# Second mixer: the softmax weights are scaled inside the turn, by a diagonal of reciprocal sums

## What is computed

```python
q = rmsnorm(q.reshape(B, S, N_HEADS, HEAD_DIM), q_gain)
k = rmsnorm(k.reshape(B, S, N_HEADS, HEAD_DIM), k_gain)
...
s = jnp.einsum('bqhd,bkhd->bhqk', qb, kb).astype(jnp.float32) * scale + bias
valid = (c * CHUNK + kpos - pad) >= 0
s = jnp.where(valid[None, None], s, NEG_INF)
p = jax.nn.softmax(s, axis=-1)
return jnp.einsum('bhqk,bkhd->bqhd', p.astype(vb.dtype), vb)
```

## Time and profile before

| what | value |
|---|---|
| median of 3 runs | 1830.04 us (1828.27 to 1830.62) |
| the profiled execution, its own time | 1829.55 us |
| its span | 1827.7 us |
| busy share: TensorE, weight load, VectorE, ScalarE | 96%, 70%, 50%, 33% |
| mean granted TensorE clock | 0.987 of full speed |
| second mixer's attention (from the first scores to the last values) | about 1342 to 1441 us |

### The profile page before, as it was taken

The page is one execution under the profiler, slowest core; times in us unless marked ns, Lnnn a source line. Parts: engine busy times, 40 slices in busy tenths (PEclk is TensorE's granted clock), DMA queues, the critical chain, the costliest instruction groups (busy, mean ns, idle before and its releaser), DMA issues.

```text
span 1827.7 us, 19981 instructions
## 1 busy us (share of the span) xinstructions
PE 1755.2 (96%) x8340; PEld 1274.3 (70%) x8340; DVE 920.1 (50%) x1311; ACT 599.1 (33%) x900; POOL 12.5 (1%) x22
## 2 busy tenths in 40 slices
PE   7999999998999999999989999999999999999998
PEld 6777887785454445343478888887877778888886
DVE  4667864634232323232444845734577444745634
ACT  4456434442111111110143323323355333323322
POOL 0000000000000000000000000000000000000000
PEclk9999999998999999999999999999999999999999
DMA  5222225525899999999932141242310142242331
GB/s 197 93 70 70 93 75 177 190 106 217 361 422 422 421 421 421 422 420 420 398 110 93 65 143 69 65 142 93 115 70 36 57 134 87 69 138 69 101 107 58
DMA packets 93167, 330.59 MB, mean 181 GB/s; under 512 B 6176, under 2 KB 15536, under 8 KB 68368
## 3 DMA queue, kind: packets, MB, share of 16 engines
q1 hardware_dynamic: 88784, 317.81, 45.6%
q0 software_dynamic: 1984, 7.25, 1.1%
q10 hardware_dynamic: 2304, 4.20, 0.6%
HBM read 322.94 MB, written 6.29 MB: 180 GB/s over the span
## 4 chain that ended last, share of the span: by engine, by line
PE 86%; DMA 5%; DVE 4%; ACT 4%; issue 1%; SPq 0%; DVEq 0%; ACTq 0%
PE PS L1503 11%; PE PS L1504 10%; PE PS L1505 10%; PE PS L1383 10%; PE PS L1499 5%; PE PS L1500 5%; PE PS L1501 5%; PE PS L1406 5%; PE PS L1478 3%; PE PS L1479 3%; PE PS L1477 3%; PE PS L1354 2%; DMA rawz<-in_w_up_experts 2%; PE PS L1355 2%; PE PS L1416 2%; PE PS L1576 2%
## 5 line engine op out<-in xcount | busy, mean ns | idle before, releaser
L2198 DVE TENSOR_TENSOR lo<-raw,hi 128x2048 fp32r<-128x2048 f32 (+2 forms) x142 | 254.2, 1794 | 317.8 <-ACT hi L1798 317.4
L1798 ACT CAST hi<-raw 128x1024 fp32r<-128x1024 f32 (+2 forms) x144 | 216.9, 1513 | 297.5 <-PE PS L1505 112.3
L1503 PE MATMUL PS<-xh_ffn,hi 128*128 128x512 f32 x576 | 225.0, 391 | 0.9 <-DVE SG L2409 0.9
L1505 PE MATMUL PS<-xh_ffn,lo 128*128 128x512 f32 x576 | 224.2, 389 | 0.0
L1504 PE MATMUL PS<-xl_ffn,hi 128*128 128x512 f32 x576 | 224.1, 389 | 0.0
L1383 PE MATMUL PS<-raw,XG 128*64 128x512 f32 x416 | 140.2, 601 | 5.0 <-DVE YL L2175 2.8
L1503 PEld LDWEIGHTS PS<-xh_ffn,hi 128*128 128x128 f32 x576 | 108.1, 188 | 23.6 <-issue 1.3
L1505 PEld LDWEIGHTS PS<-xh_ffn,lo 128*128 128x128 f32 x576 | 108.1, 188 | 22.5
L1504 PEld LDWEIGHTS PS<-xl_ffn,hi 128*128 128x128 f32 x576 | 108.2, 188 | 22.1
L2168 DVE TENSOR_TENSOR HF<-SG,PS 128x512 f32<-128x512 f32 x16 | 17.3, 1078 | 183.5 <-PE PS L1383 183.5
L1383 PE MATMUL PS<-rawz,XG 128*64 128x512 f32 x400 | 88.9, 593 | 2.9 <-DMA rawz<-in_w_up_experts 2.9
(11 more groups left out here) (481 smaller groups left out, 3499.1 us busy)
## 6 DMA issues: line engine op xcount, KB each, us to landing
raw<-in_w_in SPq DMA_DIRECT2D x26, 1024.0 KB, 5.1
raw<-in_w_gate_experts SPq DMA_DIRECT2D x26, 1024.0 KB, 15.6
raw<-in_w_up_experts SPq DMA_DIRECT2D x26, 1024.0 KB, 14.4
rawz<-in_w_up_experts SPq DMA_DIRECT2D x26, 1024.0 KB, 12.9
rawz<-in_w_down_experts SPq DMA_DIRECT2D x26, 1024.0 KB, 14.0
raw<-in_w_down_experts SPq DMA_DIRECT2D x24, 1024.0 KB, 13.3
rawz<-in_w_gate_experts SPq DMA_DIRECT2D x24, 1024.0 KB, 16.0
raw<-in_ffn_w_down SPq DMA_DIRECT2D x20, 1024.0 KB, 5.0
```

The source lines that it names most:

```text
L1503: e.matmul(o, h[:, kk, c], xh[:, k, :], start=s0, stop=False)
L1505: x = e.matmul(o, l[:, kk, c], xh[:, k, :], start=False, stop=s1)
L1798: e.copy(q.hi[:, a:b], q.raw[:, a:b]).then_inc(*a_hi((u, 0) if part == 0 else u))
L2198: e.tensor_tensor(q.lo[:, a:b], q.raw[:, a:b], q.hi[:, a:b].bitcast(F32), ALU.subtract).then_inc(*v_lo(key))
```

## The change

The exponentials in `s2` stay as they are. `m2_weights(n)` now writes four diagonal tiles of 128x128, `DG`, one to a head: the identity times the reciprocal of the row's sum. `m2_turn` is no longer a `transpose` with the identity but a plain `matmul` of the same block with the head's `DG` tile, so the block comes out turned and each query's column scaled. All tiles are float32. The list of steps is the same.

```diff
+        DG = [[at(f"DG{i}{q}", o, [128, 128]) for q, o in enumerate(os)]
+              for i, os in enumerate(((94.25, 94.75, 95.25, 142.5), (143, 21, 20.25, 18.75)))]
...
                 for hh in range(4):
                     pe.wait_ge(v_m2, ("w", n, hh))
-                    x = e.transpose(PS[:, b, hh * 128:hh * 128 + 128], s2[n % 2][:, hh, kb * 128:kb * 128 + 128], ident)
+                    x = e.matmul(PS[:, b, hh * 128:hh * 128 + 128], s2[n % 2][:, hh, kb * 128:kb * 128 + 128], DG[n % 2][hh][:, :],
+                                 start=True, stop=True)
...
             def m2_weights(n):
-                W = (4 - n // 2) * 128
-                s = s2[n % 2][:, :, 0:W]
                 c = S4[:, 16 * (n % 2):16 * (n % 2) + 16]
                 dve.wait_ge(a_m2, ("exp", n, 3))
                 e.reciprocal(c[:, 12:16], c[:, 8:12]).then_inc(*v_m2(("rl", n)))
                 dve.wait_ge(v_m2, ("rl", n))
                 for q in range(4):
-                    e.tensor_tensor(s[:, q, :], s[:, q, :], c[:, 12 + q:13 + q].broadcast_to([128, W]),
-                                    ALU.mult).then_inc(*v_m2(("w", n, q)))
+                    e.tensor_scalar(DG[n % 2][q][:, :], ident, c[:, 12 + q:13 + q], None, ALU.mult).then_inc(*v_m2(("w", n, q)))
```

## The result

The changed kernel takes 1833.28 us (median of 18 runs, 1830.68 to 1838.32), the kernel before 1829.72 us beside it. The ratio is 1.0023, with a 95% interval of 1.0016 to 1.0030: slower by 4.2 us (2.9 to 5.5) by the ratio, 3.6 us by the medians.

A forecast was written before the change was run, and what follows sets the result against it. TensorE was taken to bound the kernel: 80 added records cost it 8.9 us, 4.6 of them fall into its gaps, leaving +4.3 us on the median 1830.04, so 1834.3 us; range 1831.1 to 1838.9 us.

The forecast's parts named there:

- What bounds the kernel: In the attention TensorE bounds, with 4.7 us of idle time; what VectorE is spared is worth little.
- The price of one block: In the turn a product has two records, a transpose one; 80 more at 0.111 us add 8.9 us on TensorE.
- The rule of the Trainium skill: Rival in the turn: three added records' time per block, 26.6 us more, 1851.9 us; chance 0.03.
- group 1: Turn of 16 blocks: +1.78 us goes into TensorE's 1.99 us gap before the scores of group 3; cost 0.
- The price of a diagonal: On VectorE, 32 `tensor_scalar` 128 wide at 241 ns replace multiplications of up to 684 ns; costed at nothing but two places.
- Group by group: Over the turns of groups 0 to 7, 4.6 of the 8.9 us fall into TensorE's gaps; cost +4.3 us.
- Group 5: Its turn grows 0.89 us, 0.81 of it into a wait that VectorE's lighter weights help close; cost 0.1 us.
- The 3.0 us before the last FFN stay: TensorE's 3.0 us gap there stays, as what is waited for starts from TensorE's last output product.
- Nothing is absorbed: Rival: ScalarE's copies move back with longer turns and TensorE's gaps reopen; +8.9 us, 1838.9 us; chance 0.11.
- VectorE was the hidden bound: Rival, weights of group 1 to scores of group 3: earlier exponentials close all 4.7 us of gaps, 1825.3 us; chance 0.05.
- Too little to be told, by the clock: Rival: TensorE's clock doesn't fall behind the 3.0 us gap, 1.45 us less, 1832.9 us; chance 0.27, including group-sum errors.

The follow-up runs named there:

- e1: Changed kernel with the old transpose by the identity, VectorE still writing diagonals and no longer scaling; ratio 0.9997 to the kernel before.
- e2: Kernel before with its transposes made plain float32 products by the identity, VectorE scaling as before; median 1833.64 us, ratio 1.0020.
- e3: Changed kernel with each of the 80 products made twice; median 1851.47 us, ratio 1.0118 to the kernel before.
- e5: Kernel before with ScalarE's copies of turned blocks put ahead of its rounding of weights in groups 1, 2 and 3; median 1826.11 us, ratio 0.9978.
- e4: The changed kernel once more, unaltered, for its profile; a single run, 1835.56 us.
- e6: Kernel before with ScalarE's copies ahead of its rounding, and VectorE taking over three of the 20 copies; median 1826.26 us, ratio 0.9980.

## Why the prediction was right

By its own steps:

- **What bounds the kernel.** Right, and shown: VectorE's part alone is worth 0.48 us of the stretch and nothing that the runs can tell (e1), TensorE's part alone costs what the whole change costs (e2: the stretch 86.87 us against 86.88).
- **The price of one block.** 0.111 us to a record from the rows of another line, two records instead of one. The turn has 160 records, and 160 more cost 0.1085 us each (e3). The operand being a diagonal, or another one for each head, costs nothing: with the identity it is the same (e2).
- **The rule of the Trainium skill** against which it was weighed ("TensorE: Matmul & The Clock Gate", Terms: the transpose mode 4 times faster for float32) gave, as the prediction's estimate, 26.6 us more on TensorE. Measured is about twice, not four times: group 1's 16 blocks take 1370.84 - 1367.35 = 3.49 us as products, where they took 1.66 us as transposes; the trace does not agree with it for this pair of instructions.
- **The price of a diagonal.** The term that was off: 241 ns foretold, 281 ns measured (279 to 289), inside the bounds. The proportion between 32 and 512 wide did not hold. The 128-wide `tensor_scalar` (281 ns) is hardly cheaper than the 128-wide multiplications at L2818 were (285 ns), and a narrow group's four take 0.88 us where they took 0.90. As VectorE's time hides, it cost nothing.
- **Group by group.** All seven stretches came within 0.1 us, group 1's full 1.78 us hidden in the gap among them. The reason given for that gap was incomplete: the prediction has ScalarE busy with exponentials before its copies, but the last 0.94 us before them (1370.48 to 1371.42 us) went into a rounding of weights, and e5, which moves that rounding, halves the gap. Group 5 cost 0.18 instead of 0.1 us; e2 shows that this has nothing to do with VectorE's weights, whose help I had put in there: with the old, long weights ScalarE is done with group 6's exponentials in time too, and its copy waits 0.52 us for TensorE's turned block (0.53 us in the changed kernel). The step was right in its sum, wrong in one of its reasons and incomplete in another.
- **The 3.0 us before the last FFN stay.** Right in all nine profiles.
- **The rivals.** "Nothing is absorbed" fell with the changed profile itself, where 8.9 us of added records cost 4.36 us, and "VectorE was the hidden bound" with e1. "Too little to be told, by the clock" is right in part: the fall was missing in the first profile of the change and there in the second, and half of the change's runs show a high mean clock (last section), so on average it may have taken some tenths of a microsecond off the cost.
- **The number.** Foretold +4.3 us, 1834.3; measured +4.2 by the ratio and +3.6 by the medians, 1833.28. The interval, 2.9 to 5.5 us, reaches below the 3.7 us that the prediction wanted for a difference; that the ratio came out above it is partly luck. What bears the forecast out is the stretch, 4.36 us in one pair of profiles and 86.90 - 82.50 = 4.40 us in the other.

## What to carry to other kernels

Before work is moved from one engine to another, ask which of the two is waited for: here VectorE was spared 6.5 us and waited for TensorE instead, while TensorE, at the end of the chain, paid 4.4 of its 8.9 us. A float32 turn done as a plain product costs two records where the transpose costs one, so a scale is not free in it. And read whose copies the bound engine waits for: putting ScalarE's copies ahead of its rounding, with no work moved at all, made the kernel 2.2 to 5.9 us faster than before (e5), faster than both kernels that were compared.

## What was not expected of the hardware

Behind one and the same idle gap of 2.98 us, with the same kernel, TensorE's granted clock was once 1.00 and once 0.66 in the 5 us that follow (the change and its repeat; 0.66 lies between the two levels, so part of the 5 us was at 1.2 GHz), and the price is 1.5 us: 363.0 against 361.5 us to the end. In six of nine profiles it fell. The start of the stretch goes with the clock too: up to 1355 us the mean granted clock is 0.98 in the three profiles that start it latest (e1, e4, e6, 1358.54 to 1358.73 us) and 0.99 in the other six (1355.95 to 1357.60).

Single runs say the same. The change's nine runs with a mean clock of 0.989 or more took 1830.68 to 1832.96 us, the nine below it 1833.59 to 1838.32. And the kernel seems to shift the odds, though it doesn't decide a single run: 0.989 or more stands in 9 of 18 runs of the change, 3 of 9 of e2 and 5 of 9 of e5, the three kernels of which a profile without the fall exists, but in 1 of 37 of the kernel before (run beside the experiments), 1 of 11 of e6, none of 10 of e1 and none of 4 of e3. Why is not shown. So a change of 0.2% is read from the stretch in the trace, and from many runs, not from two spans.
